# An fp32 network on one core: nearly all up panels of its perceptrons go through seven block products, two panels overlapping, and a transfer that adds makes one block sum

## What is computed

```python
h = h + jnp.square(jax.nn.relu(_rms_norm(h, norm_ff_g[l]) @ ff_w1[l])) @ ff_w2[l]      # FF: 1024 -> 4096 -> 1024

def swiglu(x, w_gate, w_up, w_down):                                                   # GLU0, GLU1: 1024 -> 2816 -> 1024
    return (jax.nn.silu(x @ w_gate) * (x @ w_up)) @ w_down
```

## Time and profile before

| | |
|---|---|
| time, median of 3 | 1963.46 us |
| the profiled execution: its own time / its span | 1964.29 us / 1962.5 us |
| granted TensorE clock in the span | 0.995 of full |
| PE busy | 98% |
| VectorE / ScalarE / GpSimd busy | 57% / 41% / 17% |
| transfers | 179.83 MB, mean 92 GB/s |

### The profile page before, as it was taken

The page is one execution under the profiler, slowest core; times in us unless marked ns, Lnnn a source line. Parts: engine busy times, 40 slices in busy tenths (PEclk is TensorE's granted clock), DMA queues, the critical chain, the costliest instruction groups (busy, mean ns, idle before and its releaser), DMA issues.

```text
span 1962.5 us, 29944 instructions
## 1 busy us (share of the span) xinstructions
PE 1928.8 (98%) x12504; PEld 1281.4 (65%) x12504; DVE 1124.7 (57%) x1547; ACT 810.1 (41%) x1313; POOL 339.4 (17%) x355
## 2 busy tenths in 40 slices
PE   8999999999999999999999999999999999999997
PEld 5655655657676654886567666648766586666576
DVE  6666786656477642245767765523565668656224
ACT  6443411445355531133545544312464545444222
POOL 1011111410034320024011511100500124211001
PEclk9999999999999999999999999999999999999999
DMA  7211200232312322322230323323111123232321
GB/s 251 86 65 65 79 29 22 86 129 87 129 64 87 126 99 99 108 108 87 68 120 30 129 87 129 108 93 144 44 65 47 41 86 108 87 129 87 121 94 44
DMA packets 28241, 179.83 MB, mean 92 GB/s; under 512 B 2961, under 2 KB 7185, under 8 KB 7185
## 3 DMA queue, kind: packets, MB, share of 16 engines
q1 hardware_dynamic: 27312, 170.93, 24.5%
q10 hardware_dynamic: 512, 4.94, 0.7%
q0 software_dynamic: 288, 2.10, 0.3%
HBM read 175.86 MB, written 2.10 MB: 91 GB/s over the span
## 4 chain that ended last, share of the span: by engine, by line
PE 67%; DVE 1%; ACT 1%; issue 0%; ACTq 0%; DVEq 0%
PE psum_a L422 17%; PE psum_a L424 17%; PE psum_a L423 17%; PE psum_b L422 4%; PE psum_b L424 4%; PE psum_b L423 4%; PE psum_b L559 2%; PE psum_b L1171 1%; PE psum_a L1125 0%; PE psum_a L1190 0%; PE psum_b L570 0%; PE psum_a L1238 0%; PE psum_a L1245 0%; PE psum_den L1171 0%; PE psum_b L850 0%; PE psum_b L722 0%
## 5 line engine op out<-in xcount | busy, mean ns | idle before, releaser
L2015 DVE SCALAR_TENSOR_TENSOR W_PARTS<-W,W_PARTS 128x2048 f16<-128x2048 f32 x111 | 255.2, 2301 | 306.3 <-ACT W_PARTS L1346 306.2
L1346 ACT ACTIVATE W_PARTS<-W 128x2048 f16<-128x2048 f32 x111 | 211.0, 1904 | 275.0 <-PE psum_a L424 272.7
L422 PE MATMUL psum_a<-U,W_PARTS 128*128 128x512 f16 (+1 forms) x808 | 301.6, 373 | 1.5 <-DVE U L2135 1.5
L423 PE MATMUL psum_a<-U,W_PARTS 128*128 128x512 f16 (+1 forms) x808 | 301.4, 373 | 0.0
L424 PE MATMUL psum_a<-U,W_PARTS 128*128 128x512 f16 (+1 forms) x808 | 301.4, 373 | 0.0
L422 PE MATMUL psum_a<-ARENA,W_PARTS 128*128 128x256 f16 (+1 forms) x860 | 269.1, 313 | 2.3 <-DVE ARENA L2668 2.3
L424 PE MATMUL psum_a<-ARENA,W_PARTS 128*128 128x256 f16 (+1 forms) x860 | 269.0, 313 | 0.0
L423 PE MATMUL psum_a<-ARENA,W_PARTS 128*128 128x256 f16 (+1 forms) x860 | 268.9, 313 | 0.0
L2975 POOL TENSOR_TENSOR ARENA<-ARENA 128x512 f16<-128x512 f32 x76 | 108.0, 1431 | 430.8 <-ACT ARENA L1480 430.7
L424 PEld LDWEIGHTS psum_a<-U,W_PARTS 128*128 128x128 f16 x808 | 79.1, 98 | 90.4
L422 PEld LDWEIGHTS psum_a<-U,W_PARTS 128*128 128x128 f16 x808 | 79.1, 98 | 87.7 <-issue 4.1
(11 more groups left out here) (376 smaller groups left out, 4044.7 us busy)
## 6 DMA issues: line engine op xcount, KB each, us to landing
W<-weights SPq DMA_DIRECT2D x159, 1024.0 KB, 4.8
CON<-const ACTq DMA_DIRECT2D x1, 3071.5 KB, 12.9
X<-x_in SPq DMA_DIRECT2D x4, 256.0 KB, 4.0
X<-x_in SPq DMA_DIRECT2D x1, 1024.0 KB, 8.0
U<-dft POOLq DMA_DIRECT2D x1, 1024.0 KB, 5.8
ARENA<-dft POOLq DMA_DIRECT2D x1, 1024.0 KB, 5.4
U<-mem_in ACTq DMA_DIRECT2D x1, 1024.0 KB, 4.8
y_out<-U SPq DMA_DIRECT2D x2, 512.0 KB, 2.9
```

What stands on the lines that cost most here:

```text
L422: nc.tensor.matmul(out, left(0), right(0), start=first, stop=False, skip_group_check=goes_on)
L423: nc.tensor.matmul(out, left(0), right(1), start=False, stop=False, skip_group_check=goes_on)
L1346: nc.scalar.activation(HOMES[home_of[g]][:, 0, :], W[g % 2][:, :], ACT.Copy, scale=W_SCALE).then_inc(sem("panel_high"), 1)
L2015: nc.vector.scalar_tensor_tensor(out=home[:, 1, :], in0=W[g % 2][:, :], scalar=W_SCALE, in1=home[:, 0, :], op0=ALU.mult, op1=ALU.subtract) ...
```

## The change

FF has now one plain panel (up 2) and 13 of seven (up 3 to up 15); each GLU has one plain panel (gate 1) and 19 of seven (up 1, gate 2, up 2, ..., gate 10, up 10). Every second panel of seven keeps its blocks in `ODD_BLOCKS`, which lies over `W_PARTS`, and has its own three PSUM banks; q7 and q4 of a panel run inside the next one. The fourth block sum is no VectorE instruction any more: GpSimd issues a transfer (`third_sum`) that adds block A11 from HBM to A21 in `W`. In a GLU the gate tiles get their Silu on ScalarE (`gate_silu`). GpSimd's `rescale` of the activations is cut into four portions among the panels. Two semaphores are merged into others.

```diff
+        PART = lambda at, i: SQ[:, 3 if i == 1 and at % 2 else i, :]
+        ODD_BLOCKS = block_parts(W_PARTS[:, :, :].rearrange("p a b -> p (a b)")[:, 0:7 * BLOCK])
...
+                self.plain, self.sevens = (("gate", 1), [("up", 1)]) if gated else (("up", 2), [])
+                for j in range(2 if gated else 3, groups):
+                    self.sevens += [("gate", j), ("up", j)] if gated else [("up", j)]
...
+        def last_read(M, at):
+            if at % 2 == 0:
+                return sem("tile_21"), tiles_21[M.name] + at // 2 + 1
+            return sem("gate_ready"), gates_before[M.name] + (3 if M.gated else 1) * (at // 2 + 1)
...
# TensorE
+                def seven_panel(at):
...
+                    released.append((sem("seven_done"), seven_at[n, "q4"]))
+                    if at % 2:
+                        last_in[0] = last_in[1] = g
                     pe.wait_ge(sem("blocks_low"), 2 * n + 1)
+                    if at > 1:
+                        pe.wait_ge(*last_read(M, at - 2))
+                    one_of_seven(at, "q1")
                     pe.wait_ge(sem("blocks_low"), 2 * n + 2)
                     pe.wait_ge(sem("v_low"), 4 * MLPS[M.norm] + 1)
+                    if at > 1:
+                        pe.wait_ge(sem("tile_added"), 3 * (n - 2) + 2)
...
+                    one_of_seven(at, "q5")
+                    if at:
+                        sixth(at - 1)
+                    one_of_seven(at, "q2")
                     pe.wait_ge(sem("part_read"), 3 * n + 1)
                     pe.wait_ge(sem("v_low"), 4 * MLPS[M.norm] + 2)
+                    one_of_seven(at, "q6")
+                    if at:
+                        seventh(at - 1)
                     pe.wait_ge(sem("part_read"), 3 * n + 2)
+                    one_of_seven(at, "q3")
...
# ScalarE
             def rest_high(M, key):
-                act.wait_ge(sem("block_sum"), 4 * n + 4)
+                act.wait_ge(sem("idft_and_s3_landed"), 16 * (n + 2))
...
+                first, second = M.sevens[0:2]
+                raw_high(M, first)
+                sums_high(M, first)
+                rest_high(M, first)
+                plain_tile(M, M.plain, 0)
+                raw_high(M, second)
+                plain_tile(M, M.plain, 1)
+                read_part(M, first, 0)
+                read_part(M, first, 1)
+                sums_high(M, second)
+                read_part(M, first, 2)
+                v_high(M, (V7, V4))
+                for j in range(1 if M.gated else 2):
+                    hidden_high(M, j)
...
+                for at in range(1, len(M.sevens)):
+                    key = M.sevens[at]
+                    rest_high(M, key)
+                    read_part(M, key, 0)
+                    read_part(M, key, 1)
+                    if at + 1 < len(M.sevens):
+                        raw_high(M, M.sevens[at + 1])
+                        sums_high(M, M.sevens[at + 1])
+                    if at == 1 and not M.gated:
+                        hidden_high(M, M.plain[1])
+                    if M.gated:
+                        finished(at - 1, 0)
+                        read_part(M, key, 2)
+                        finished(at - 1, 1)
+                    else:
+                        read_part(M, key, 2)
+                        tile_21(M, M.sevens[at - 1])
+                        hidden_high(M, M.sevens[at - 1][1])
+                last = len(M.sevens) - 1
+                down = panel_of[(M.name,) + M.sevens[last]] + 1
+                split(down)
+                split(down + 1)
...
# VectorE
-                nc.vector.tensor_tensor(block(3), block(3), block(0), ALU.add).then_inc(sem("block_sum"), 1)
...
+                rest_low(M, first)
+                v_made(M, src, V7)
+                block_sums(M, second)
+                raw_low(M, second)
+                sums_low(M, second)
+                v_low(M, (V7,))
+                v_made(M, src, V4)
+                add_part(M, first, 0)
+                v_low(M, (V4,))
+                for at in range(1, len(M.sevens)):
+                    before, key = M.sevens[at - 1:at + 1]
+                    more = M.sevens[at + 1:at + 2]
+                    add_part(M, before, 1)
+                    rest_low(M, key)
+                    for following in more if at > 1 else ():
+                        block_sums(M, following)
+                    add_part(M, before, 2)
...
+                    for following in more:
+                        raw_low(M, following)
+                    if at == 1 and not M.gated:
+                        hidden(M.plain[1])
+                    finish(M, before, 0)
+                    add_part(M, key, 0)
+                    for following in more:
+                        sums_low(M, following)
+                    finish(M, before, 1)
...
# GpSimd
+            def third_sum(M, at):
+                if at < len(M.sevens):
+                    key = M.sevens[at]
+                    n, g = M.seven[key], panel_of[(M.name,) + key]
+                    pool.wait_ge(sem("block_sum"), 3 * n + 1)
+                    pool.dma_start(W[g % 2][:, 3 * BLOCK:4 * BLOCK], weights[g][:, 0:BLOCK], accum_op=ALU.add)\
+                        .then_inc(sem("idft_and_s3_landed"), 16)
+
+            def mlp(M):
+                third_sum(M, 0)
+                if M.gated:
+                    hidden_low(M, 0, 1)
+                third_sum(M, 1)
+                pool.wait_ge(sem("v_made"), 4 * MLPS[M.norm] + 4)
+                if not M.gated:
+                    hidden_low(M, 0, 1, 2, 3)
+                for at in range(1, len(M.sevens) + 2):
+                    third_sum(M, at + 1)
+                    if not M.gated:
+                        if at <= len(M.sevens) + 1:
+                            hidden_low(M, 2 * at + 2, 2 * at + 3)
+                    else:
+                        if at <= 4:
+                            rescale(M.norm, range(4 * at - 4, 4 * at))
+                        hidden_low(M, at + 1)
...
-    return [_by_blocks(w) if n >= first and n % 2 else w for n, w in enumerate(panels)]
+    return [_by_blocks(w) if n >= first else w for n, w in enumerate(panels)]
```

More of the change, by code:

```diff
@@ L980, in mlp @@
                 for key in [("mean", M.norm, 1), ("sum", M.norm, 0), ("sum", M.norm, 1)][0 if M.gated else 1:]:
                     pe.wait_ge(B.freed_sem(key), B.freed_at(key))
-                before = None
-                for plain, seven in M.pairs:
-                    w, g = panel()
-                    panel_of[(M.name,) + plain] = g
-                    w = w.rearrange("p l (k c) -> p l k c", k=KT)
-                    for m in range(2):
-                        bank = reuse(A, (M.name,) + plain + (m,))
-                        for kt in range(KT):
-                            last = product(bank[:, :], lambda l: w[:, l, kt, m * P:(m + 1) * P], lambda l: U16[:, l, kt, :], kt == 0, kt == KT - 1)
-                            if before and m == 0 and kt == KT // 2 - 1:
-                                sixth(before)
-                        last.then_inc(A.done, 1)
-                        if before and m == 0:
-                            seventh(before)
-                    released[g] = A.done, A.n
-                    first_five(seven)
-                    before = seven
+                w, g = panel()
@@ new lines, in mlp @@
+                panel_of[(M.name,) + M.plain] = g
+                w = w.rearrange("p l (k c) -> p l k c", k=KT)
+                for m in range(2):
+                    bank = reuse(A, (M.name,) + M.plain + (m,))
+                    for kt in range(KT):
+                        last = product(bank[:, :], lambda l: w[:, l, kt, m * P:(m + 1) * P], lambda l: U16[:, l, kt, :], kt == 0, kt == KT - 1)
+                    last.then_inc(A.done, 1)
+                released[g] = A.done, A.n
+                spare = [(A.free[(A.n + i) % 4], (A.n + i) // 4) for i in range(2)]
@@ L1000, in mlp @@
+                seven_banks = (psum_b, [psum_den] + [A.banks[(A.n + i) % 4] for i in range(2)])
+                for at in range(len(M.sevens)):
+                    seven_panel(at)
+                before = len(M.sevens) - 1
+                pe.wait_ge(sem("tile_added"), 3 * M.seven[M.sevens[before]])
+                pe.wait_ge(*last_read(M, before - 1))
                 kept = {}
@@ L1036, in mlp @@
                         released[g] = A.done, A.n
[L1037 to L1038 removed]
+                pe.wait_ge(*last_read(M, before))
+                pe.wait_ge(sem("tile_added"), 3 * M.seven[M.sevens[before]] + 3)
                 wide = {}
@@ L1540, in mlp @@
-                split(panel_of[(M.name,) + before] + 2)
-                hidden_high(M, before[1], (0,))
-                if not M.gated:
-                    tile_21(M, before)
-                hidden_high(M, before[1], (1,))
+                first, second = M.sevens[0:2]
[5 more added lines that the diff above has]
+                plain_tile(M, M.plain, 1)
@@ L2101, in finish @@
```

(42 more changed lines are left out.)

295 lines of the change are left out of this document (145 added, 150 removed).

## The result

The changed kernel takes 2049.92 us (median of 4 runs, 2047.72 to 2058.88) against 1963.76 for the kernel before: a ratio of 1.0445, 95% interval 1.041 to 1.048. The direction was forecast, the size was not: 2000 us was predicted, the range ended at 2040. The profiled execution has a span of 2049.3 us against 1962.5. From the first split of FF to the same split of GLU0 it takes 541.8 us for 502.4, from there to the one of GLU0's end 236.9 for 212.9, and the rest behind it, in which GLU1 lies, some 25 us more.

The account below looks back on a forecast made before the run. TensorE, 98% busy, bounds the kernel before; the helpers' waits would outweigh its gain. From 1964.3 us, TensorE -28.8, FF +28.0 and both GLUs +36.4 give +35.6, 1999.9: predicted 2000 us, range 1976 to 2040.

Parts of the forecast that it names:

- TensorE's gain: All three perceptrons: fewer matmul columns save 1.2 us per converted panel, 28.8 us in all.
- FF's cycle: the written order: FF, each panel: ScalarE's and VectorE's instructions in written order take 9.60 us, above TensorE's 9.16.
- The sign that I gave for it: FF's cycles: TensorE would be seen waiting in front of q5 for `sums_low`.
- FF's cycle: GpSimd's hindrance: FF: two `hidden_low` per panel cost VectorE 1.2 us, making the cycle 10.8 us.
- my own upper bound of 1.92: FF's cycle: the most that GpSimd's two `hidden_low` could cost VectorE, 0.96 us each time.
- GLU cycles: Each GLU: a gate and up pair takes 18.5 us against TensorE's 18.3, 1.8 us over 9 pairs.
- GLU opening: Start of each GLU: TensorE stalls 8.9 us at q6 and 3.9 more at q1, 12.8 us.
- Turns: Turn to the down panels: TensorE waits for the first split, 4.9 us in FF, 3.6 in each GLU.
- The adding transfer: GpSimd's transfer making the fourth sum lands after 4.5 us; up to about 6 is hidden in steady state.
- the 2.6 us that the prediction works out beside it: The adding transfer's time by the Trainium skill: 2.0 us plus bytes by 436 GB/s; the sum some 5 us lower.
- rival C: Slow adding transfer becomes the ring with S1, `rest_high`, `rest_low`: 2035 us at 7 us, 2055 at 7.6; chance 13%.
- delays nobody who is late: GpSimd's issue of the adding transfer: under 1 us of its time, holding up nothing that is late.

Follow-up runs that it names:

- e8: The changed kernel with the edits of e2, e3 and e5 together: 1992.05 us.
- e1: The changed kernel with GpSimd's `hidden_low` on 8 of 512 columns per tile and the down products reading the high part twice: 1997.01 us.
- e7: The changed kernel with GpSimd doing `hidden_low` ahead of the next panel's adding transfer, in FF alone: 2035.76 us.
- e5: The changed kernel with GpSimd issuing the second panel's adding transfer ahead of `hidden_low` of tiles 0 and 1 in each GLU opening: 2040.29 us.
- e10: The changed kernel with q7 of the last seven panel ahead of the wait for the down panel's split: 2044.13 us.
- e3: The changed kernel with ScalarE's `rest_high` of the next panel ahead of `hidden_high` of the panel before (in GLU, the second `hidden_high`): 2021.12 us.
- e9: The changed kernel with filler matmuls that nothing reads ahead of TensorE's wait at each turn (20 in FF, 14 in each GLU): 2044.95 us.
- e11: The changed kernel with 10 filler matmuls that nothing reads ahead of q5 in FF's cycles: 2051.19 us.
- e6: The changed kernel with 28 filler matmuls that nothing reads ahead of the second seven panel's q6 in each GLU opening: 2052.92 us.
- e2: The changed kernel with `hidden_low` of all but the first and last tiles moved from GpSimd to VectorE: 2018.9 us.

## Why the prediction was wrong

The direction came out right, and by the mechanism that was forecast: VectorE's written order and GpSimd's hindrance bound the stages. The size did not. By stage, the prediction's own sum has FF 20.8 us longer (28.0 - 7.2) and each GLU 7.4 (18.2 - 10.8); measured are 39.4, 24.0 and some 25. One term was sized too small in FF, two in the GLU stages, and one effect was missing.

- **TensorE's gain, 28.8 us.** It shows nowhere by itself, since TensorE waits or runs slower. Where nothing holds it up it is there: five GLU pairs of e8 take 18.3 us, two panels of 9.16.
- **FF's cycle: the written order, 9.60 us.** Right: e1 has 9.62. The sign that I gave for it was not: TensorE waits in front of q4 for `add_part`, not in front of q5 for `sums_low`.
- **FF's cycle: GpSimd's hindrance, "I take 2 x 0.6 = 1.2".** This is the step that failed. It was 2.56, above my own upper bound of 1.92. I had let each subtraction begin beside an `add_part` that absorbs part of it, and bounded it by what one `finish` lost in the earlier trace rows; but behind the transfer both run back to back, 2.54 us, and all of it falls on S4. 1.36 us x 12 cycles = 16 us of the miss (ten cycles have such an S4; in the first and the last one other instructions pay). The whole of `hidden_low`'s hindrance, GLU stages included, is 53 us (e1) where I had some 18. The rule of the Trainium skill that I weighed (SBUF — State Buffer, "Who interferes with whom") says that a VectorE instruction with two inputs in SBUF and a GpSimd instruction that reads SBUF contend, and that the one that issues first has the shared ports for its whole length. The exclusion is borne out in both directions, by S4's 3.25 us and by e7's 2.18 us. Who was first can be read in e7 alone, where `sums_low` starts 0.6 us before `hidden_low` and keeps its length; S4's row starts 0.15 us before GpSimd's two subtractions and it waits for both, so the start of a row does not show who has the ports. I should have taken the rule without absorption, and with the order in GpSimd's queue.
- **GLU cycles, 18.5 us a pair, 1.8 us a stage.** The second step that failed. Too small: 20.3 a pair on the mean of GLU0. The waits of q1 cost 16.0 us in GLU0, 4.4 of them in the opening, so 11.6 against 1.8. Part by part: VectorE's ring without GpSimd's subtractions is 17.95 us (e1) where I had 17.3; the subtractions add 1.28 (19.23 less 17.95) where I had 1.2; and the gap behind the landing, 0.47 to 2.43 us, I had put at nothing. With `rest_high` early and `hidden_low` on VectorE most pairs take TensorE's 18.3 (e8). In the first two pairs, 21.2 and 21.3 us, GpSimd also runs its portions of `rescale`, which I had put at nothing; in e8, with the same `rescale`, the second takes 18.3. What it costs in the changed kernel no run separates.
- **GLU opening, 12.8 us.** Right in sum: 7.4 at q6 (8.9 said) and 4.4 at q1 (3.9). e5 shows that they are one budget: 5.9 us taken from the first gave 2.5 to the second.
- **Turns.** Right: 4.9 and 3.4 us for 4.9 and 3.6; e10 confirms what they wait for.
- **The adding transfer.** Its landing is 5.9 us for 4.5; the 2.6 us that the prediction works out beside it is further off. I had read only loads of 1 MB and more; the page before also has four of 256 KB (`X<-x_in`), at 4.0 us. In FF the landing is hidden, as I said of anything up to 6 us, and rival C (the transfer as the ring) is out there: ScalarE waits for a landing once, and e7 and e3 shorten the cycle with the transfer in it. In the GLU stages rival C holds in part: the landing is in the ring of the gate panels. That its issue "delays nobody who is late" was wrong: it puts `hidden_low` behind S1 and 1.5 us a cycle more onto VectorE than e7 does.
- **The clock.** Not in the prediction. At the turns it is 5 us (e9), in FF's cycles nothing (e11). In the GLU openings it falls too; what it costs there wasn't settled (e6). GLU0 grew by 24.0 us; 26.8 of waits less 10.8 of TensorE's gain are 16.0, and 8 us are left over. Four products behind the opening's wait took 2.53, 2.03, 2.16 and 2.12 us for 1.31, 3.6 us more, two of them in front of a wait that VectorE ends; how much of this lengthened the stage is not shown, and for the rest I have no count.

Against 2000 us: hindrance +35 (53 less the 18 that my cycles held: 14.4 in FF, some 3.6 in the GLU pairs), pairs without it 0.95 us too long x 18 = +17 (19.25 in e1 against TensorE's 18.3, the gap behind the landing), clock at the turns +5, openings and turns -2: 2055, for 2050 measured. That this comes out close is in part luck, for the terms overlap: e2 and e3 gain 31 and 29 us alone.
